# Second layer's input projection moved into the first layer's tail, and the first inverse norms computed within the modulation block

## What is computed

```python
def decoder_layer(x, c, ...):
    mod = jnp.dot(jax.nn.silu(c), ada_w) + ada_b          # 1024 x 6144, for the prompt and for each sample
    sh1, sc1, g1, sh2, sc2, g2 = jnp.split(mod[:, None, :], 6, axis=-1)
    h = rmsnorm(x, norms[0]) * (1 + sc1) + sh1
    aq, ak, av, af, bq, bk, bv, bg, ca, cb = split_cols(jnp.dot(h, w_in))
    logf = jax.nn.log_sigmoid((af + b_f).astype(F32))
    ...                                                    # attention (4 heads x 128)
    q_b = rope(bq, pos); k_b = rope(bk, pos) * (DKB ** -0.5)
    ...                                                    # retention (4 heads x 64)
    u = ca * jax.nn.sigmoid(cb)
    cv, conv_state = causal_dwconv(conv_ctx, u, conv_w, conv_b)      # width 31, 256 channels
    ...
    x = x + g1 * rmsnorm(mix, norms[1])
    h2 = rmsnorm(x, norms[2]) * (1 + sc2) + sh2
    up, ffn_state = causal_dwconv(ffn_ctx, jnp.dot(h2, ffn_up), ffn_conv_w, ffn_conv_b)  # width 3
    a, b = jnp.split(up, 2, axis=-1)
    f = jnp.dot(jax.nn.silu(a) * b, ffn_down)
    x = x + g2 * rmsnorm(f, norms[3])
```

## Time and profile before

| | us |
|---|---|
| median of 3 runs | 2892.43 |
| all runs | 2884.91, 2892.48, 2892.43 |
| the profiled execution | 2882.91 |
| its span, first to last instruction | 2880.4 |
| PE busy in it | 2752.8 (96%) |
| DVE busy | 1772.8 (62%) |
| ACT busy | 1190.6 (41%) |
| POOL busy | 195.0 (7%) |

### The profile page before, as it was taken

The page is one execution under the profiler, slowest core; times in us unless marked ns, Lnnn a source line. Parts: engine busy times, 40 slices in busy tenths (PEclk is TensorE's granted clock), DMA queues, the critical chain, the costliest instruction groups (busy, mean ns, idle before and its releaser), DMA issues. The chain is left out here.

```text
span 2880.4 us, 46373 instructions
## 1 busy us (share of the span) xinstructions
PE 2752.8 (96%) x18620; PEld 2440.1 (85%) x18620; DVE 1772.8 (62%) x2865; ACT 1190.6 (41%) x1925; POOL 195.0 (7%) x101
## 2 busy tenths in 40 slices
PE   6999999899999999999949999999999999999998
PEld 4888888788788899999938889887877888999997
DVE  5593445556766765676756743554667667667655
ACT  3241334544444444444422313344444445544444
POOL 1221100110000000000011210102000000000000
PEclk7999999999999999999969999999999999999999
DMA  6842223443333344232228312334333333323322
GB/s 223 250 121 60 68 67 96 118 139 95 93 97 89 94 141 147 81 96 89 70 93 226 90 43 68 88 89 132 129 91 96 95 95 96 89 79 91 95 87 86
DMA packets 439452, 302.02 MB, mean 105 GB/s; under 512 B 28061, under 2 KB 402437, under 8 KB 438438
## 3 DMA queue, kind: packets, MB, share of 16 engines
q1 hardware_dynamic: 433205, 289.39, 34.2%
q10 hardware_dynamic: 6033, 9.67, 1.1%
HBM read 276.07 MB, written 23.78 MB: 104 GB/s over the span
## 5 line engine op out<-in xcount | busy, mean ns | idle before, releaser
L1761 PE MATMUL tslot<-h_hi,w_hi 128*128 128x260 f32 (+1 forms) x2496 | 674.9, 325 | 9.6 <-DVE h_lo L2565 6.2
L1761 PE MATMUL tslot<-h_hi,w_lo 128*128 128x260 f32 (+1 forms) x2496 | 667.0, 322 | 0.0
L1761 PE MATMUL tslot<-h_lo,w_hi 128*128 128x260 f32 (+1 forms) x2496 | 664.9, 321 | 0.0
L1761 PEld LDWEIGHTS tslot<-h_hi,w_hi 128*128 128x128 f32 x2496 | 416.4, 190 | 55.2 <-issue 9.9
L1761 PEld LDWEIGHTS tslot<-h_hi,w_lo 128*128 128x128 f32 x2496 | 415.4, 189 | 37.8
L1761 PEld LDWEIGHTS tslot<-h_lo,w_hi 128*128 128x128 f32 x2496 | 415.6, 190 | 37.2
L1732 ACT ACTIVATE w_hi<-w_raw 128x1024 fp32r<-128x1024 f32 x292 | 307.1, 1052 | 330.0 <-PE tslot L2187 308.4
L1736 DVE TENSOR_TENSOR w_lo<-w_raw,w_hi 128x1024 fp32r<-128x1024 f32 x276 | 336.1, 1218 | 3.1 <-ACT w_hi L1732 3.1
L2650 DVE TENSOR_TENSOR cat<-cat,tslot 128x512 f32<-128x512 f32 (+1 forms) x320 | 220.4, 690 | 185.7 <-PE tslot L2187 185.0
L2187 PE MATMUL tslot<-f_hi,w_hi 128*128 128x260 f32 (+1 forms) x1056 | 283.7, 323 | 6.9 <-DVE w_lo L1736 4.2
L2613 DVE SCALAR_TENSOR_TENSOR bufs<-bufs,vecs 128x512 f32<-128x512 f32 x176 | 132.0, 750 | 252.5 <-ACT bufs L2442 252.3
(11 more groups left out here) (370 smaller groups left out, 3798.7 us busy)
## 6 DMA issues: line engine op xcount, KB each, us to landing
w_raw<-in_ffn_up_dram SPq DMA_DIRECT2D x176, 512.0 KB, 3.9
w_raw<-in_ffn_down_dram SPq DMA_DIRECT2D x88, 512.0 KB, 3.8
x_res<-in_ada_w_dram SPq DMA_DIRECT2D x64, 512.0 KB, 5.3
w_raw<-in_w_in_dram SPq DMA_DIRECT2D x48, 512.0 KB, 4.6
w_raw<-in_w_o_dram SPq DMA_DIRECT2D x32, 512.0 KB, 5.5
x_hold<-x_res SPq DMA_DIRECT2D x2, 4128.0 KB, 17.0
x_res<-x_hold SPq DMA_DIRECT2D x2, 4128.0 KB, 12.7
a_raw<-in_ada_w_dram SPq DMA_DIRECT2D x4, 2048.0 KB, 22.4
```

Of the source, the lines that this page charges most:

```text
L1761: last = pe.matmul(out[:, at + a:at + b], w[:, kk, :], x[:, kk, t0 + a:t0 + b], start=(kk == 0 and first), stop=(kk == KD - 1 and w is w_lo))
```

## The change

The projection of the second layer is no block any more. `block_project(k)` remains for the first layer, and `block_tail` of the first layer goes on, behind its last down tiles, with 11 projection tiles for token half 0 and 11 for half 1 (`next_item`, `next_place`, `next_hook`; ACT `next_read`, DVE `next_on_dve`, `next_gate`, `next_rope`). The norm of the second token half (`ends[1]`) is spread over the tiles of half 0. Low parts of half 0's weights are made by DVE, those of half 1 by POOL. Of the 62 taps 32 are done there and 30 in the second layer's mixer, three in a step (`TAPS_STEP`). All 24 pairs of modulation parts for the second layer are now made in the first layer's tail, in units 4 to 11, 13 to 20 and 23 to 30 of the second token half; the turn comes one unit after the product, and DVE reads eight blocks at a time (i = 6, 11, 16). The misc bank holds eight turned blocks, so that products 8 and 16 wait for that reading.

In the head the token sums, the inverse norm, its diagonal and its spread stand inside `block_modulation`, the last piece of `ada_w` is loaded and multiplied in two, and the normalization's low parts of odd blocks go to POOL in place of the even ones.

```diff
@@ block_modulation
+        PIECES = [(b, 0, W) for b in range(BLOCKS - 1)] + [(BLOCKS - 1, 0, W // 2), (BLOCKS - 1, W // 2, W)]
-            for b in range(BLOCKS):
...
+            for n, (b, low, high) in enumerate(PIECES):
+                if b == 2:
+                    pe.wait_ge(summed, KD - 1)
+                    pe.wait_ge(scaled, 4)
+                    pe_token_sums(k, pe, st, acc, True, True).then_inc(sums_ready, 1)
...
-                if b >= 1:
-                    turn(b - 1)
-                if b == 2:
-                    pe.wait_ge(summed, KD - 1)
-                    pe_token_sums(k, pe, st, acc, True, True).then_inc(sums_ready, 1)
-            turn(BLOCKS - 1)
+                if n >= 1:
+                    turn(n - 1)
+                if n == BLOCKS - 1:
+                    pe.wait_ge(diag_ready, 1)
+                    pe_spread(k, pe, diag, rb)
+            turn(BLOCKS)
@@
-POOL_LOWS = (0, 2, 4, 6)
+POOL_LOWS = (1, 3, 5, 7)
-TAPS_EARLY = 50
+TAPS_EARLY = (50, 32)
@@ block_tail
+        MODS, MW, MOD_BATCH = MOD_PARTS // 2, 2 * P, 8
+        mod_at = lambda b: 4 + b + b // MOD_BATCH + (b >= 2 * MOD_BATCH)
+        MOD_AT = {divmod(mod_at(b), 2): b for b in range(MODS)}
+        MOD_TURN = {divmod(mod_at(b) + 1, 2): b for b in range(MODS)}
@@ SP
+                for m in range(3, PROJECT):
+                    load_next(0, m)
...
+                    if m == 8:
+                        sp.wait_ge(ends[1].dve_added, KD)
+                        sp.wait_ge(ends[1].samp, 3)
+                        sp.dma_start(k.x_hold.rearrange("p (a b) -> p a b", b=NT), k.x[:, :, :]).then_inc(x_held, 16)
+                load_next(1, 0)
+                sp.wait_ge(ends[1].dve_low, KD)
...
+                for m in range(1, PROJECT):
+                    load_next(1, m)
@@ PE
+                elif b % MOD_BATCH == 0:
+                    pe.wait_ge(mod_read, b // MOD_BATCH)
-                        if not final and 2 <= i <= 2 + MODS:
-                            mod_hook(i)
+                    if hf and not final and kk == 4:
+                        if (i, half) in MOD_TURN:
+                            mod_turn(MOD_TURN[i, half])
+                        if (i, half) in MOD_AT:
+                            mod_product(MOD_AT[i, half])
@@ PE
+            if not final:
+                for hf in range(2):
+                    for m in range(PROJECT):
+                        n = next_item(hf, m)
+                        st.ready(pe, n)
...
+                        half_product(pe, k, st, n, out, at, hf, next_hook(hf, m)).then_inc(st.used, 1)
@@ POOL
+                for m in range(PROJECT):
+                    st.low(pool, next_item(1, m))
@@ ACT
-                    if not final and hf and 2 <= i < 2 + MODS:
-                        act.wait_ge(mod_done, i - 1)
-                        act.activation(mod_row[i % 2], misc[0][:, 0:MW], ACT.Copy).then_inc(row_ready, 1)
+                    if not final and hf and (i, 0) in MOD_AT:
+                        mod_rows(MOD_AT[i, 0])
                     read_out(hf, i, 1)
+                    if not final and hf and (i, 1) in MOD_AT:
+                        mod_rows(MOD_AT[i, 1])
@@ DVE
+                next_gate(1, 0)
+                dve.wait_ge(dve_free, 3)
+                for n in range(12):
+                    nlink(conv_tap(k, dve, n))
+                next_gate(1, 1)
+                dve.wait_ge(dve_free, 4)
+                at = 12
+                for i in range(4):
+                    for n in range(at, at + 5):
+                        nlink(conv_tap(k, dve, n))
+                    at += 5
+                    next_rope(1, i)
@@ block_mixer
+        TAPS, TAPS_STEP = 2 * CONV_W - TAPS_EARLY[L], 1 + 2 * L
...
-                if 1 <= p <= 2 * CONV_W - TAPS_EARLY:
-                    clink(conv_tap(k, dve, TAPS_EARLY + p - 1))
+                if p >= 1:
+                    for n in range(TAPS_STEP * (p - 1), min(TAPS_STEP * p, TAPS)):
+                        clink(conv_tap(k, dve, TAPS_EARLY[L] + n))
```

More of the change, by code:

```diff
@@ L307, in _, with turn @@
         def _(pe):
-            def turn(b):
-                pe.wait_ge(row_ready, b + 1)
-                if b >= 2:
-                    pe.wait_ge(added, b - 1)
-                for j in range(TW):
-                    last = pe.matmul(tp[b % 2][:, 9 * j:9 * j + 9], mrow[b % 2][:, P * j:P * j + P], const(k, "pick")[:, 0:9], start=True,
+            def turn(n):
+                _, low, high = PIECES[n]
+                pe.wait_ge(row_ready, n + 1)
+                if n >= 2:
+                    pe.wait_ge(added, n - 1)
+                for j in range((high - low) // P):
+                    last = pe.matmul(tp[n % 2][:, 9 * j:9 * j + 9], mrow[n % 2][:, P * j:P * j + P], const(k, "pick")[:, 0:9], start=True,
                                      stop=True)
@@ L350, in _ @@
                 act.activation(sq[kk % 3][:, :], k.x[:, kk, :], ACT.Square).then_inc(squared, 1)
-            for b in range(BLOCKS):
-                act.wait_ge(product_done, b + 1)
-                if b >= 2:
-                    act.wait_ge(turned, b - 1)
-                act.activation(mrow[b % 2][:, :], mp[b % 2][:, :], ACT.Copy).then_inc(row_ready, 1)
-                if b == 1:
+            for n, (b, low, high) in enumerate(PIECES):
+                act.wait_ge(product_done, n + 1)
+                if n >= 2:
+                    act.wait_ge(turned, n - 1)
+                act.activation(mrow[n % 2][:, 0:high - low], mp[n % 2][:, 0:high - low], ACT.Copy).then_inc(row_ready, 1)
+                if n == 1:
                     ahead.high(act)
@@ new lines, in turn_states, with turn_taps @@
+            def turn_states():
+                pe.wait_ge(side_loaded, 48)
+                next_freed(pe, 0, 10)
+                for half in range(2):
+                    for j in range(2):
+                        last = pe.matmul(misc[0][:, 240 * j + 120 * half:240 * j + 120 * half + 120],
+                                         crow[:, half, P * j:P * j + P], ident[0:120, 0:120], start=True, stop=True)
+                last.then_inc(n_ctx_turned, 1)
+            def turn_taps():
+                pe.wait_ge(n_rows_loaded, 48)
+                for n in range(2):
+                    pe.matmul(misc[1][:, 324 + 88 * n:412 + 88 * n], vrow[0:88, n, :], ident[0:88, 0:88], start=True, stop=True)
@@ L2657, in ffn @@
                     taps(hf, i, 0)
+                    if hf and not final and i in (6, 11, 16):
+                        mod_out((i - 6) // 5)
                     if u >= 4 and u % 4 == 0:
@@ L2728, in _ @@
             st.low(dve, item_down(PAIRS - 1, 1))
+            if not final:
+                st.low(dve, N_ITEMS)
             gather(PAIRS - 1, 0)
@@ L2733, in _ @@
                     ends[1].dve_acc(dve, m - 1)
+                if m == 6 and not final:
+                    st.low(dve, N_ITEMS + 1)
             if final:
@@ L2754, in _ @@
             else:
-                take(ends[1].on_dve(dve), 2 * KD + 6)
+                next_on_dve()
 def trunk(nc, dram):
```

457 lines of the change are left out of this document (332 added, 125 removed).

## The result

The changed kernel takes 2942.3 us (median of four runs, 2937.2 to 2945.6), the kernel before beside it 2892.4: a ratio of 1.0181, 95% interval 1.0166 to 1.0196. Slower was forecast, by 26 us; it is 50 us by the medians and 62.3 us between the two profiled executions (spans 2880.4 and 2942.7). The profiled execution of before lay at the low end of its runs, that of after 2.4 us above its median. The time lies 4 us above the range.

A forecast was written before the change was run, and what follows sets the result against it. PE was taken as the bound, busy 2752.8 of 2880.4 us. Terms −45 +23 +27 +4 +3.5 +5 +10.5 −2 gave +26; added to the median 2892.4 that made 2918, leaned to 2915 us; range 2880 to 2938.

The forecast's parts named there:

- part 4: Clock in the tail: three drops to the lower level behind new waits, 1.7 us each, +5; bounds 0 and 20.
- part 6: Head: most of PE's 3.28 us wait for the diagonal goes, the spread only changes place; −2, between −6 and +1.
- part 5: Second layer's mixer: three taps a step make PE wait for the state update in seven steps; +10.5, between 3 and 20.
- part 3: First tail: turns one unit after products make PE wait for row copies, +27; late weights +4; products 8 and 16, +3.5.
- rival (a): Tail: the turns cost nothing, so parts 3 and 4 vanish; sum −10, 2883 us; chance alone 0.14.
- Part 1 and 2: Boundary to the second mixer shortened, gain 45 us (−45); 16 more product pairs inside the tail, cost +23.
- (b): Boundary gives 15 us more as POOL and DVE hardly meet; sum +11, 2901 us; chance alone 0.12.
- (d): Boundary gives less, half 1 starting 10 us later; 2925 us; chance 0.22 together with rival (c).
- Rival (c): Tail: the clock falls at each long turn wait, +15 more, 2930 us; chance 0.22 together with (d).
- the moved odd low parts of POOL cost nothing: Head: POOL's moved odd low parts add no time, as neither DVE nor PE waits for them first.
- Part 3, the reading of eight blocks: Tail: products 8 and 16 wait until DVE has read eight turned blocks; about +3.5 for both, between 0 and 6.
- the 9.5 us: Median of the three timed runs before lay 9.5 us above the profiled execution; the sum was added to that median.

The follow-up runs named there:

- e2_copy_first: The changed kernel with ACT's row copy of each modulation block put ahead of the unit's reading: 2894.5 us, 1.0024 of before.
- e7_even: The changed kernel with one load for the last modulation weight piece and POOL making the even blocks' low parts in the first normalization: 2939.4 us, measured once.
- e10_seven: The changed kernel with one last-piece load, earlier row copies, block readings and tile load, later mixer taps, POOL's even blocks, six low parts on DVE: 2859.3 us, 0.9893.
- e8_dve_lows: The changed kernel with the low parts of tiles 5 to 10 of half 1 made by DVE between its taps, not by POOL: 2938.4 us, 1.0171.

## Why the prediction was wrong

The forecast failed in two terms of its sum, the clock of part 4 (18.8 us measured in the tail, 5 put in) and the head of part 6 (+10 measured, −2 put in); with the smaller error of part 5 (14.6 against 10.5) they are 30 of the 36 us between +26 and +62.

- **Direction and main mechanism: right.** The step of part 3, that nothing covers the row copy when its turn comes one unit later, was found as worked out; taking the waits away brings the time to 0.24% of before (1.0024). The sum, 29.1 us in 18 waits against 27 and 4 for late weights, agrees partly by luck: the plain waits and those in second units were 5 us less than forecast, and what late weights and squares put on top was 7 and not 4. The rival (a), turns that cost nothing, fell by the trace and by that experiment.
- **Part 1 and 2: right within 1 us.** −45 stands against −45.9, each step of the boundary within 1 us, and 23 for the products against the 23 that e2_copy_first leaves for them. The rivals (b) and (d) fell with the boundary.
- **Part 4, the clock: mis-sized, and the largest error.** "Three drops by 1.7 us" were in fact eight new ones by 2.1 and an old one grown by 1.7, 18.8 us against 5 (and 6 more in the mixer, where none was put in). Seven of the eight lie behind turns, one behind the reading of eight blocks. Two steps failed. I took the length of the waits as 1.9 and below for all, though part 3 itself had late weights coming on top of that (1.35 us, so 3.2 in all), and the earlier trace rows have a wait of 2.95 with the lower clock behind it; and I overlooked ACT's squares, which make others that long. And I took one row of 2.27 us as proof that shorter waits do nothing, where 1.68, 1.96 and 2.08 each had a drop behind them. Rival (c) named the direction and gave 2930; it was the case that came, with two more errors on top.
- **Part 6, the head: wrong in sign.** +10 against −2. I counted the split load as nothing, but each half is an issue of its own on SP, as long as that of a whole piece (5.3 and 5.9 us), and the block waits for SP's last issue: 5 us. The row that shows SP busy until the block's end was there, four such loads in 17.63 us in the timeline of before, and wasn't read. And "the moved odd low parts of POOL cost nothing" was wrong by 3.4 us. The gain of 2 isn't found either: with both put right the first mixer starts at 228.6 (e7_even) or 227.0 (e10_seven), and at 226.8 before. PE's wait for the diagonal, 3.28 us before, is 0.46 in the changed kernel, but 2.14 in these two.
- **Part 5, the mixer: 14.6 against 10.5.** The waits are 8.9 (10.5 forecast), but two of them brought the clock down, the first of 2.38 us (3.4 lost) and one of 1.40 (1.7 lost), which the sum had left out.
- **Part 3, the reading of eight blocks:** 5.1 against 3.5, within its bounds, and a drop of 1.7 behind the second, counted in part 4.
- **The median.** 62 us between profiled executions are 50 between medians, since that of before was the shortest of its runs. I had noted the 9.5 us, and added the sum to the median without asking what makes single runs shorter; the last section has a sign of it.

The range missed because its upper end took the clock (20) without the head and the mixer. The larger errors were all of one sign: what the clock loses behind added waits, and two changes in the head that were put at nothing.

## To carry to other kernels

A new wait of a microsecond or two of a saturated PE has two prices, its own length and what the clock loses behind it; here the second was not quite half of the first (12 to 14.5 us to 29.1), and waits that come on top of each other (a late load, a norm's squares) are the ones to look for, as they get long enough. When a hand-over is moved to be one unit away, put the producer's step where its engine waits anyway: the same 24 blocks cost 43.6 us less once ACT copied each row ahead of its wait for the unit. A load split in two is two issues on its queue: look who waits for the queue.

## What was unexpected of the hardware

The clock's fall isn't set by the length of one wait alone. A wait of 2.27 us in the kernel before had no drop behind it; the same wait of the changed kernel did, and cost 3.4 us:

```profile
646.75 1.87 PE L1782 MATMUL tmisc<-consts,rc 128*128 128x1 f32 x8 [2.23 <-DVE w_lo L1728]
```

```profile
647.00:649.00 2.00, 2.00 (x10) 2.00 (x11) 1.70 (x5) 0.29 (x1) 0.00 (x0) 0.50 0.53 150
```

And a wait of 1.68 us (at 1078.75) had a drop behind it, with 0.76 in the window from 1079 to 1081, where one of 1.69 (at 1128.11) had none.

```profile
1079.00:1081.00 2.00, 2.00 (x22) 1.21 (x22) 0.00 (x0) 0.00 (x0) 0.00 (x0) 0.76 0.03 8
```

The clearest pair is one and the same wait in two runs whose tails have the same code, the changed kernel first, then e8_dve_lows, and a window behind each:

```profile
1227.85 0.61 PE L2347 MATMUL tmisc<-consts,rows_lo 128*128 128x9 f32 x4 [2.40 <-ACT rows_lo L2605]
1227.76 0.61 PE L2350 MATMUL tmisc<-consts,rows_lo 128*128 128x9 f32 x4 [2.40 <-ACT rows_lo L2608]
```

```profile
1230.00:1232.00 2.00, 2.00 (x19) 2.00 (x18) 0.00 (x0) 0.00 (x0) 0.00 (x0) 1.00 0.57 165
1230.00:1232.00 2.00, 2.00 (x11) 2.00 (x10) 0.00 (x0) 0.00 (x0) 0.00 (x0) 0.50 0.62 174
```

Both are 2.40 us, with the same matmuls ahead and behind, and only the second has a drop. The long wait before it, near 1208, goes the other way: 2.08 us with a drop in the changed kernel, 2.15 without one in e8_dve_lows. Nearly every drop of the tails costs 1.7 us, or twice that.

That fits with the Trainium skill (TensorE: Matmul & The Clock Gate, "What's actually happening"), by which the number of matmuls at the lower clock differs between runs of the same kernel; that this is why single runs of one kernel differ by some 10 us here was not tested.

Behind the first, a 2048 KB load keeps SP's queue for 5.3 to 6.6 us, and half of it for 5.3 and 5.9: the time doesn't go with the bytes. The half load has as many rows (8 on each of 128 partitions), of half the length; whether the number of rows or something else sets the time was not tried. The Trainium skill (Perfetto Trace Analysis, "What 'DMA-bound' means") says that this window is the making of descriptors and that large ones matter, with which the rows agree: the same 2048 KB in shorter rows took SP twice as long (11.27 us against 5.29).
